# First adaptation of the second block summed by VectorE inside the first feed-forward, and the feed-forward's squares moved to ScalarE

## What is computed

```python
# first block, each of 2 layers
x = x + mixed @ w_out[l]
h = rms_norm(x, ln2_gain[l])
x = x + jnp.square(jax.nn.relu(h @ w_up[l])) @ w_down[l]      # 1024 -> 4096 -> 1024
...
# second block, first layer
def adaln(cond, w, b):
    m = jax.nn.silu(cond) @ w + b                             # w: 1024 x 3072
    return jnp.split(m, 3, axis=-1)
shift, scale, gate = adaln(c[:, None, :], w_ada, b_ada)
cshift, cscale, cgate = adaln(c_ctx, w_ada, b_ada)
```

## Time and profile before

| what | us |
|---|---|
| median of 3 runs (lowest to highest) | 1077.51 (1077.5 to 1077.96) |
| span of the profiled execution, first to last instruction | 1076.1 |
| PE busy in the span | 1051.7 (98%) |
| PEld, DVE, ACT busy | 900.5, 751.0, 549.1 |
| compression and retention of layer 0 (74 to 106 us), PE busy | 31.5 of 32 |
| feed-forward of layer 0 (161 to 345 us): PE, DVE, ACT busy | 183.7, 106.6, 89.3 of 184 |

### The profile page before, as it was taken

How to read it: one execution, slowest core, us unless ns; L and a number is a source line. 1 busy time by engine, 2 the same in 40 slices (tenths; PEclk the granted TensorE clock), 3 DMA queues, 4 the chain that set the end, 5 groups by cost and what they waited for, 6 DMA issues and landing times. The chain is left out here.

```text
span 1076.1 us, 17324 instructions
## 1 busy us (share of the span) xinstructions
PE 1051.7 (98%) x6788; PEld 900.5 (84%) x6788; DVE 751.0 (70%) x1442; ACT 549.1 (51%) x993; POOL 63.4 (6%) x80
## 2 busy tenths in 40 slices
PE   8999999999999999999999999999999999999996
PEld 7877889899988886888998899888886687989865
DVE  5766757655556576777788888789898945824765
ACT  5543845544445454764444544452657833623563
POOL 1000000000000000001000000020051301000000
PEclk9999999999999999999999999999999999999998
DMA  9758056565564657325856566593326233943200
GB/s 344 263 197 344 3 157 195 162 201 191 192 196 163 196 196 266 120 84 185 185 196 196 160 199 197 189 305 133 110 93 260 78 118 107 257 140 118 60 21 40
DMA packets 55477, 183.33 MB, mean 170 GB/s; under 512 B 21092, under 2 KB 33764, under 8 KB 35940
## 3 DMA queue, kind: packets, MB, share of 16 engines
q1 hardware_dynamic: 55396, 182.22, 51.8%
HBM read 179.31 MB, written 2.90 MB: 169 GB/s over the span
## 5 line engine op out<-in xcount | busy, mean ns | idle before, releaser
L257 DVE TENSOR_TENSOR w_lo<-ring,w_hi 128x1024 fp32r<-128x1024 f32 x259 | 316.2, 1223 | 179.8 <-ACT w_hi L242 176.2
L242 ACT CAST w_hi<-ring 128x1024 fp32r<-128x1024 f32 x259 | 270.9, 1054 | 318.0 <-PE banks L313 317.5
L313 PE MATMUL banks<-f_hi,w_hi 128*128 128x256 f32 x512 | 144.0, 281 | 0.0
L313 PE MATMUL banks<-f_hi,w_lo 128*128 128x256 f32 x512 | 143.8, 281 | 0.0
L313 PE MATMUL banks<-f_lo,w_hi 128*128 128x256 f32 x512 | 143.8, 281 | 0.0
L313 PE MATMUL banks<-w_hi,u_hi 128*128 128x512 f32 x256 | 100.1, 391 | 0.0
L313 PE MATMUL banks<-w_hi,u_lo 128*128 128x512 f32 x256 | 99.9, 390 | 0.0
L313 PE MATMUL banks<-w_lo,u_hi 128*128 128x512 f32 x256 | 99.9, 390 | 0.0
L313 PEld LDWEIGHTS banks<-f_hi,w_hi 128*128 128x128 f32 x512 | 96.4, 188 | 0.7 <-DVE f_lo L444 0.2
L313 PEld LDWEIGHTS banks<-f_lo,w_hi 128*128 128x128 f32 x512 | 96.5, 188 | 0.5
L313 PEld LDWEIGHTS banks<-f_hi,w_lo 128*128 128x128 f32 x512 | 96.5, 188 | 0.0
(11 more groups left out here) (421 smaller groups left out, 2167.9 us busy)
## 6 DMA issues: line engine op xcount, KB each, us to landing
ring<-in_w_up SPq DMA_DIRECT2D x32, 1024.0 KB, 5.2
ring<-in_w_down SPq DMA_DIRECT2D x32, 1024.0 KB, 5.1
ring<-in_w_in SPq DMA_DIRECT2D x23, 1024.0 KB, 5.2
ring<-in_ab_ada SPq DMA_DIRECT2D x12, 1024.0 KB, 5.9
ring<-in_cd_ada SPq DMA_DIRECT2D x12, 1024.0 KB, 5.2
ring<-in_cd_in SPq DMA_DIRECT2D x12, 1024.0 KB, 5.6
ring<-in_w_out SPq DMA_DIRECT2D x8, 1024.0 KB, 7.5
ring<-in_ab_in SPq DMA_DIRECT2D x16, 512.0 KB, 4.8
```

The lines of the kernel that those rows point to most:

```text
L242: nc.scalar.copy(w_hi[:, n % PARTS, :], part_source(key, q)).then_inc(hi_ready, 1)
L257: nc.vector.tensor_tensor(w_lo[:, n % PARTS, :], part_source(key, q), w_hi[:, n % PARTS, :].bitcast(F32), ALU.subtract).then_inc(part_read ...
L313: mm = nc.tensor.matmul(dst, a, b, start=first_one and i == 0, stop=last_one and i == 2, skip_group_check=shares_bank)
```

## The change

The three adaptation slabs per layer leave the ring's order in the compression stages, with their products, copies, turns and bias adds. Instead the twelve halves of `ab_ada` are loaded among the 32 halves of layer 0's feed-forward (behind halves 1, 3, 5, 8, 10, 13, ...). DVE multiplies each 128 x 512 chunk by a column of the condition and adds it to `ada_sums` (96 instructions, two for each part of weights in most places). PE adds the 128 partitions up by a matmul with one column of `minus_half`, 48 of them: 40 in the middle of the last down slab, 8 behind its end. One DVE instruction scales by -2 and adds the bias. In both layers' feed-forwards ACT squares the relu itself, in place of DVE.

```diff
-LAYER_SLABS = [("w_in", W_IN_SLABS), ("ada_turn", 1), ("cmp_k", 1), ("cmp_v", 1), ("small", 1), ("ada_small", 1),
-               ("ada_mix", 1), ("w_out", 2), ("ffn", 16)]
+LAYER_SLABS = [("w_in", W_IN_SLABS), ("cmp_k", 1), ("cmp_v", 1), ("small", 1), ("w_out", 2), ("ffn", 16)]
...
+ADA_SLABS = 3 * D // BANK
+ADA_BEHIND = [1 + m * 29 // (2 * ADA_SLABS) for m in range(2 * ADA_SLABS)]
...
+        def adapt_on_vector(dve, sums_of, done):
+            n = 0
+            for m, i in enumerate(ada_at):
+                for kk in range(KC // 2):
+                    k = m % 2 * (KC // 2) + kk
+                    w = ring[:, i % SLOTS, kk * BANK:(kk + 1) * BANK]
+                    if kk == 0:
+                        half_here(dve, i)
+                    for v in range(2):
+                        to, factor = sums_of[:, m // 2, v, :], cond[:, k, v:v + 1]
+                        if k == 0:
+                            last = nc.vector.tensor_scalar(to, w, factor, None, ALU.mult)
+                        else:
+                            dve.wait_ge(done, n - 1)
+                            last = nc.vector.scalar_tensor_tensor(out=to, in0=w, scalar=factor, in1=to, op0=ALU.mult,
+                                                                  op1=ALU.add)
+                        last.then_inc(done, 1)
+                        n += 1
+                        if kk == KC // 2 - 1 and v == 1:
+                            dve.wait_ge(done, n)
+                            dve.sem_inc(half_used, 1)
+                        yield
+        def ops_behind(half, part):
+            return 2 * sum((half, part) in ((b - 1, 1), (b, 0), (b, 1), (b + 1, 0)) for b in ADA_BEHIND)
+        def sum_conditions(pe, sums_of, s, to):
+            for f in range(4):
+                for v in range(2):
+                    n = 2 * (4 * s + f) + v
+                    mm = nc.tensor.matmul(to[:, n:n + 1], sums_of[:, s, v, f * P:(f + 1) * P], minus_half[:, 0:1],
+                                          start=True, stop=True)
+            return mm
...
-                    adapt_products(pe, ada_key, 0, 7)
...
-                    pe.wait_ge(kept, 1)
-                    turn_conditions(adapted(0), banks[:, 7, :]).then_inc(turned, 1)
...
-                    pe.wait_ge(ada_ready, 1)
-                    adapt_products(pe, ("ada_small", layer), 0, 7, signal=False)
...
-                adapt_products(pe, ada_key, 0, ADA)
...
-                turn_conditions(adapted(1), banks[:, ADA_TURNED, 0:16])
                 turn_heads(2)
-                turn_conditions(adapted(2), banks[:, ADA_TURNED, 16:32]).then_inc(mix_turned, 1)
...
                             mm.then_inc(part_used, 1)
+                            if not beside and i == 2 * FFN_GROUPS - 1 and q == 1:
+                                pe.wait_ge(relu_ready, FFN_GROUPS)
+                                pe.wait_ge(adapted, 16 * (ADA_SLABS - 1))
+                                for s in range(ADA_SLABS - 1):
+                                    sum_conditions(pe, ada_sums, s, ada_columns)
...
                     if not beside:
-                        keep_busy(0, 4)
+                        pe.wait_ge(adapted, 16 * ADA_SLABS)
+                        sum_conditions(pe, ada_sums, ADA_SLABS - 1, ada_columns).then_inc(columns_ready, 1)
+                        keep_busy(1, 4)
                         return
...
                         nc.scalar.activation(relu[:], hidden_banks(g), ACT.Relu).then_inc(relu_ready, 1)
+                        act.wait_ge(relu_ready, g + 1)
+                        if g >= 1:
+                            act.wait_ge(u_ready, g)
+                        nc.scalar.activation(square[:], relu[:], ACT.Square).then_inc(square_ready, 1)
...
-                        dve.wait_ge(relu_ready, g + 1)
-                        nc.vector.tensor_tensor(square[:], relu[:], relu[:], ALU.mult).then_inc(square_ready, 1)
                         dve.wait_ge(high_ready, g + 1)
```

More of the change, by code:

```diff
@@ L101, in slab_plan @@
 def slab_plan():
-    halves, first, first_part, n_parts = [], {}, {}, 0
+    halves, first, first_part, half_at, ada_at, n_parts = [], {}, {}, {}, [], 0
     uses = [((name, layer), name, layer * n, n) for layer in range(DEPTH) for name, n in LAYER_SLABS]
@@ L120, in slab_plan @@
             for c0 in (0, HALF):
+                half_at.setdefault(key, []).append(len(halves))
                 if name == "ffn":
@@ L127, in slab_plan @@
                     halves.append((name, at + (W_IN_AT[i] if name == "w_in" else i), c0, HALF))
-    return halves, first, first_part
+                if key == ("ffn", 0) and len(half_at[key]) - 1 in ADA_BEHIND:
+                    m = len(ada_at)
+                    ada_at.append(len(halves))
+                    halves.append((ADA_NAMES[0], m // 2, m % 2 * HALF, HALF))
+    return halves, first, first_part, half_at, ada_at
 def build_program(nc, dram, out):
-    plan, first, first_part = slab_plan()
+    plan, first, first_part, half_at, ada_at = slab_plan()
     with ExitStack() as ctx:
@@ L209, in load_first_part, with load_behind @@
             sp.dma_start(ring[:, 0, cols], dram[name][at, :, cols]).then_inc(first_parts_here[q], 16)
-        def load_behind(sp, key, n_slabs, halves=2):
-            for i in range(first[key], first[key] + halves * n_slabs):
+        def load_behind(sp, key, n_slabs, between=0):
+            for i in range(first[key], first[key] + 2 * n_slabs + between):
                 load_half(sp, i + SLOTS)
@@ L223, in part_source @@
         def part_source(key, q):
-            return ring[:, (first[key] + q // 2) % SLOTS, (q % 2) * PART:(q % 2 + 1) * PART]
+            return ring[:, half_at[key][q // 2] % SLOTS, (q % 2) * PART:(q % 2 + 1) * PART]
         def split_hi(act, key, q):
@@ L237, in split_hi @@
             elif q % 2 == 0:
-                half_here(act, first[key] + q // 2)
+                half_here(act, half_at[key][q // 2])
             if n >= PARTS:
@@ L2201, in _ @@
                 def _(sp):
-                    for i in range(first["ada_turn", layer], first["ada_mix", layer]):
+                    for i in range(first["cmp_k", layer], first["w_out", layer]):
                         load_half(sp, i + SLOTS)
@@ L2420, in compress_and_retain @@
             kept_sums = sums[:, 40:40 + NR]
-            ADA, ADA_TURNED = 6, 5
-            ada_key = ("ada_mix", layer)
             def faded_of(h):
@@ L2811, in _ @@
                         advance(taps, 2)
+                        advance(adaptation, ops_behind(2 * i + 1, 1))
                     advance(taps)
@@ L2822, in _ @@
                                                            op0=ALU.mult, op1=ALU.add).then_inc(x_done, 1)
+                    if not beside:
+                        dve.wait_ge(columns_ready, 1)
+                        nc.vector.scalar_tensor_tensor(
+                            out=ada[:, 0, :, :], in0=ada_columns.rearrange("p (f v) -> p f v", v=2), scalar=-2.0,
+                            in1=feats2[:, 0:4 * ADA_SLABS].unsqueeze(2).broadcast_to([P, 4 * ADA_SLABS, 2]), op0=ALU.mult,
+                            op1=ALU.add)
                     if beside:
```

46 lines of the change are left out of this document (18 added, 28 removed).

## The result

The changed kernel takes **1090.0 us** (median of four runs, 1089.06 to 1097.14) where the kernel before took 1077.5: a ratio of 1.0128, 95% interval 1.0099 to 1.0157. It is slower, as forecast, by 12.5 us where 8.1 were forecast, and two hundredths of a microsecond above the range's upper end of 1090.0. The four runs differ by the mean granted clock of TensorE: 0.992, 0.990, 0.988 and 0.980 go with 1089.27, 1089.06, 1090.77 and 1097.14 us.

What follows compares the result with a forecast made beforehand. PE's list was taken to bound the kernel: -8.2 (compression and retention) + 0 (squares) + 1.8 (DVE) + 8.6 + 1.7 (sums) = +3.9, plus 4.2 for the clock: 1077.5 to 1085.6 us, range 1079 to 1090.

Steps and rivals of the forecast that it cites:

- That PE's list sets the time: Whole kernel: PE busy 98% of the span; work taken from DVE or ACT is worth nothing by itself.
- costed at 1.8: Start of layer 0's feed-forward: PE waits for DVE's low parts behind the added sums, +1.8 us, bounds 0.5 and 4.
- forecast 8.6 and 1.7: Layer 0's feed-forward: 40 sums inside the last down slab +8.6 us, 8 behind it +1.7 us.
- The clock falls in the 40 sums: Last down slab, layer 0's feed-forward: one-column sums lower the granted clock, +4.2 us, 1085.6 us in all; chance 0.45.
- The rival in which the clock stays: The 40 sums: clock not lowered, 1077.5 + 3.9 = 1081.4 us, own range 1079 to 1084; chance 0.37.
- I take +4.2: the lower pace for 3 us of sums, and 1.2 of products: End of layer 0's feed-forward: sums after the fall take as long again, products behind lose time; +4.2 us.
- the bounds of 1.4 and 9: Cost of the clock's fall: 1.4 if weight loads keep pace; 6.4 + 2.7 = 9 with a fall after 2.2 us.
- So each layer gives back 4.1 us of 8.0: Compression and retention: PE loses 8.0 us of work a layer, 4.1 comes back, the rest idles; -8.2 us in all.
- The first step: Compression, first removed product: PE starts the latents' products at about 75.4 in place of 76.5, 1.1 of 1.85 us.
- forecast 92.2: Retention, third removed product: PE starts the values at 92.2 in place of 96.34, 4.1 us so far.
- 2 us of it right ahead of attention: Both layers: of the removed work's time that PE idles, 2 us stands ahead of attention's first product.
- Squares at 0: Feed-forward squares moved to ACT: worth 0 in layer 1; in layer 0 they make room for DVE's sums.

Runs made afterwards that it cites:

- the spread sums: Kernel after, with the 40 sums in five groups of 8 behind parts of down slabs 6 and 7 in place of one row: 1086.9 us.
- the runs with 40 and 128 columns: Kernel after, each of the 48 sums multiplying its weights by 40 or 128 equal columns in place of one: 1089.9 us and 1086.25 us.
- the kernel with fillers and spread sums: Kernel after with the 40 sums in five groups of 8, plus 2 and 6 filler matmuls in PE's waits in both attention stages: 1082.5 us.
- the kernel without the sums: Kernel after without the 48 sums on PE, DVE's products kept, second block's first adaptation wrong: 1073.6 us.

## Why the prediction was right in direction and short by 4.4 us

- **That PE's list sets the time, so that work moved to DVE is worth nothing by itself and work moved onto PE costs in full**: right. DVE's 96 operations cost 2.4 us, at the waits near the start, where they were costed at 1.8; PE's sums cost 8.5 (at clock 1.00, in the spread sums) and 1.70, forecast 8.6 and 1.7.
- **The clock falls in the 40 sums** (0.45, the likeliest): right, and the runs with 40 and 128 columns show it to be from how few columns each sum multiplies. The rival in which the clock stays, 1081.4, is the kernel with fillers and spread sums: 1082.5.
- **"I take +4.2: the lower pace for 3 us of sums, and 1.2 of products"**: the step that failed. The clock fell 3.35 us after the sums began, so 5.2 us of them took twice as long, not 3; the products lost 1.6. That is 6.9 us in the profiled run, inside the bounds of 1.4 and 9 but 2.7 over the value taken, and most of the 4.4 that the forecast was short. The guess at the moment of the fall was the weak point: 3 us of sums left put it 5.6 us behind the first sum, and the five profiles with such a row have it at 2.6 to 4.5. The rows at hand had a pause of 2.2 us ahead of the fall, which I used for the upper bound only. That loads slow with the clock, read from the start's pace, was right: 0.112 us a load before the fall, 0.21 behind it.
- **"So each layer gives back 4.1 us of 8.0"**: 3.72 and 3.73 measured, 0.75 us short in all. The first step was exact (the products of the latents began at 75.44 with the later start of 0.43 us taken off; forecast 75.4). The values began at 92.65 so counted, forecast 92.2; that is all of the miss.
- **What was no term of the sum**: that the attention stages, thinned out, lose the clock in some runs. The prediction did write that PE would idle there, "2 us of it right ahead of attention" (2.03 measured), and treated the idle time as free. Eight profiles have the thinned stages without fillers; in five of them the clock falls there, at 1.9 to 3.7 us for a fall in layer 1. None of the three with the adaptation's products in place and none of the three with fillers shows one. I put the spread of 3.6 us of the kernel without the sums down to it, and with it the 0.75 us by which the median of 1090.0 lies above the profiled run, whose attention stages had no fall; where the clock fell in the runs without a profile was not recorded, so these two are not shown.
- **Squares at 0**: nearly. The time of the kernel before with that edit alone can't be told from no change, but PE's products gain 0.3 us in layer 0 and 0.7 in layer 1, short waits that the prediction's rows didn't show. They also make room, which was named and not priced: with them on DVE the kernel is 12.9 us slower.
- **The range's upper end**, 1090, was the upper bound of the likeliest case. With the fall at its bound of 9 the sum gives 1090.4; a range that took all terms at their upper bounds would have reached further.

## What to carry to other kernels

When products are taken out of a stage that waits, count what is left there against the matmul clock, and not only how long the waits are; fillers that fit in the waits cost nothing here and kept the clock. When partitions are to be added up on TensorE, make the data the moving operand, with a narrow column of ones as weights and several groups of output partitions side by side: here that took 3.8 us where the data as weights took 10.2 and also lost the clock. If the data must be the weights, 128 equal columns cost hardly more than one (1.78 against 1.70 us for the eight at the end) and kept the clock in the 40.

## What the runs showed of the hardware

- TensorE can be busy without a pause and still be granted half its clock: 10.40 of 10.40 us at 0.50, with one column a product, and 8.40 of 8.40 with 40; with 128 columns 8.85 us at 1.00. Eight one-column sums between dense products kept it at 1.00, five times over.
- Weight loads slow down with the clock: two in 0.2125 us at 1.00 (1.70 us for eight sums), 0.42 at 0.50. The Trainium skill, page TensorE: Matmul & The Clock Gate, section LDWEIGHTS, has one load of 128 columns at 107 ns; the first agrees, the second is twice that.
- A multiply-add on DVE of 128 x 512 shows a mean length of 748 ns in the groups, while two in a row start 0.66 us apart, so lengths of neighbours overlap in these rows. The forecast's 0.67 us from start to start gave the right load: DVE is busy for 156 us of the stage, forecast 158.
